# Reading the moving operand of the down products in runs from two halves

## The chip, the core and the metric

The kernel runs on one core of one Trainium2 chip. The metric is the device time of one execution in microseconds (us): lower is better. TensorE (PE in the profile) does the matrix products, with its weight loads shown apart as PEld; VectorE is DVE, ScalarE is ACT, and SyncE (SP) issues the loads from HBM.

## The reference

The reference sends 256 tokens of width 1024 through two models of two layers each. Each layer of the first has a feed-forward block, an attention mixer and a second feed-forward block; each layer of the second has a mixer (a recurrence, a retention and a spatial gate) and a feed-forward block with a causal convolution of width 3. The change touches the last product of each feed-forward block:

```python
def swiglu(x, w_gate, w_up, w_down):
    return (jax.nn.silu(x @ w_gate) * (x @ w_up)) @ w_down

def conv_ffn(h, w_up, conv_w, conv_b, w_down):
    u = h @ w_up                                   # width 2 * 2816
    c = conv_b + sum(conv_w[j] * shifted(u, j))    # three shifts along the tokens
    gate, val = jnp.split(c, 2, axis=-1)
    return (jax.nn.silu(gate) * val) @ w_down      # (256, 2816) @ (2816, 1024)
```

(The sum over the shifts is shortened here.) There are four blocks of the first kind and two of the second. All values are float32.

## The kernel before

`ffn_phase` is one feed-forward block, plain or convolutional (then `conv` is given). Both matrices are cut along the 2816 hidden units into 11 chunks of 256 units. For each chunk, `hidden` (lines 528 to 547) computes gate and up for its 2 x 128 units and all 256 tokens, with the weights stationary and the 256 tokens moving. `down` multiplies the chunk's activations by its 256 rows of the down weights: 128 tokens are stationary, 512 of the 1024 output columns move. It adds into four PSUM banks, `acc[t][half]`, for 2 blocks of 128 tokens and 2 halves of 512 output columns; they stay open over all 11 chunks. VectorE adds the finished banks to the residual `x`.

Every product is done three times, since float32 operands are split in a rounded high part and a low part of the type float32r: high x high, high x low, low x high. That is `matmul3`, lines 85 to 91, so nearly all matmuls of the profile carry the line L89, L90 or L91. Each of the three loads its stationary operand again. A chunk has 2 x 2 x 8 x 3 = 96 matmuls of 256 columns in `hidden` and 2 x 2 x 2 x 3 = 24 of 512 columns in `down`. With 6 blocks of 11 chunks there are 6336 of the first and 1584 of the second (1056 in the plain blocks, 528 in the convolutional).

The order on each engine is the order of the code. TensorE does `hidden` of chunk i + 1 and then `down` of chunk i. ScalarE makes the high parts of arrived weights (L348 gate and up, L358 down) and the activation function (L363), VectorE the low parts (L426, L443) and the product (L462 to L466). SyncE loads the next chunk as soon as the buffer that its weights first arrive in is free. TensorE waits in `down` for `down_split` and `act_ready`, which VectorE counts up.

A float32 value takes 4 bytes, so 512 moving columns are 2048 bytes in a row of one partition of SBUF, and the result is 2048 bytes in a row, a whole PSUM bank of the partition. The addresses of the operands differ between the plain blocks and the convolutional ones.

Of the kernel before, what the change touches and what calls it, by code (L numbers as in the profile page):

```python
# [84 lines left out]
def matmul3(pe, out, lhs, rhs, start, stop):  # L85

    pe.matmul(out, lhs[0], rhs[0], start=start, stop=False)  # L89
    pe.matmul(out, lhs[0], rhs[1], start=False, stop=False)  # L90
    return pe.matmul(out, lhs[1], rhs[0], start=False, stop=stop)  # L91
# [69 lines left out]
def turn_tensor(pe, c, banks, ph):  # L161

    for b in range(2 * NT):
        t, k0 = b // 2, (b % 2) * 4
        if ph.prev and t:
            keep_clock(pe, c, 2 if b % 2 else 9)
        pe.wait_ge(ph.s["h_ready"], ph.n0["h_ready"] + b + 1)
        for k in range(k0, k0 + 4):
            last = pe.transpose(c.ps[banks[b]][:, (k - k0) * P:(k - k0 + 1) * P], c.h[:, t, k * P:(k + 1) * P], c.ident)
        last.then_inc(ph.s["turned"], 1)  # L170
    if ph.prev:
        keep_clock(pe, c, 4)
# [85 lines left out]
def ffn_phase(nc, c, phase, mem, gain, weights, factor=0.5, conv=None, turn_banks=FIRST_BANKS, same_as=None):  # L258
# [9 lines left out]
    def split(tensor, part, slot):  # L268
        return tuple((tensor[slot][lo][part] if part < 2 else tensor[lo][slot]).rearrange(
            "p (k n) -> p k n", k=KT if part < 2 else 2) for lo in range(2))  # L270

    w = [[split(mem.parts if part < 2 else mem.down_parts, part, slot) for slot in range(2)] for part in range(3)]
    hT = (hT_parts[:, 0], hT_parts[:, 1])
    act_high, act_low = act_parts[:, 0], act_parts[:, 1]
# [6 lines left out]
    acc = [[c.ps[4 + 2 * t + half] for half in range(2)] for t in range(NT)]  # L281
# [242 lines left out]
    def tensor(pe):  # L524
        if ph.start:
            ph.start.shared_ready(pe)
        turn_tensor(pe, c, turn_banks, ph)

        def hidden(i, slot, first=False):
            for f in range(2):  # L530
                bank = c.ps[2 * slot + f]
                for part in range(2):
                    if first and not ph.prev and f == 0:

                        pe.wait_ge(s["gu_split" if part else "first_low"], n0["gu_split" if part else "first_low"] + 1)
                    elif first and not ph.prev:
                        pe.wait_ge(s["gu_split"], n0["gu_split"] + 2)
                    else:
                        pe.wait_ge(s["gu_split"], n0["gu_split"] + i * 2 + part + 1)
                    high, low = w[part][slot]  # L540
                    for k in range(KT):
                        if first and f == 0 and part == 0 and k in (0, KT // 2):
                            pe.wait_ge(s["hT_ready"], n0["hT_ready"] + (3 if k == 0 else 4))
                        last = matmul3(pe, bank[:, part * S:(part + 1) * S],
                                       (high[:, k, f * P:(f + 1) * P], low[:, k, f * P:(f + 1) * P]),
                                       (hT[0][:, k, :], hT[1][:, k, :]), k == 0, k == KT - 1)
                last.then_inc(s["hidden_ready"], 1)

        def down_bank(slot, f, t, half, start, stop):
            toks, cols = slice(t * P, (t + 1) * P), slice(half * 512, half * 512 + 512)  # L550
            return matmul3(pe, acc[t][half][:], (act_high[:, slot, f, toks], act_low[:, slot, f, toks]),
                           tuple(part[:, f, cols] for part in w[2][slot]), start, stop)

        def down(i, slot, first=False):
            pe.wait_ge(s["down_split"], n0["down_split"] + i + 1)
            for f in range(2):
                pe.wait_ge(s["act_ready"], n0["act_ready"] + i * 2 + f + 1)
                for t in range(NT):
                    for half in range(2):
                        last = down_bank(slot, f, t, half, first and f == 0, False)  # L560
            last.then_inc(s["down_done"], 1)

        hidden(0, 0, first=True)
        hidden(1, 1)
        down(0, 0, first=True)
        hidden(2, 0)
        down(1, 1)
        with pe.Fori(0, LOOPS - 1) as i:
            hidden(i * 2 + LOOP0, 1)
            down(i * 2 + LOOP0 - 1, 0)  # L570
            hidden(i * 2 + LOOP0 + 1, 0)
            down(i * 2 + LOOP0, 1)
        hidden(LAST - 1, 1)
        down(LAST - 2, 0)
        hidden(LAST, 0)

        pe.wait_ge(s["down_split"], n0["down_split"] + LAST)
        pe.wait_ge(s["act_ready"], n0["act_ready"] + 2 * LAST)
        for t in range(NT if conv is not None else 1):
            for half in range(2):  # L580
                for f in range(2):
                    down_bank(1, f, t, half, False, False)
        pe.wait_ge(s["down_split"], n0["down_split"] + N_CHUNK)
        pe.wait_ge(s["act_ready"], n0["act_ready"] + 2 * N_CHUNK)
        for half in range(2):
            down_bank(0, 0, 0, half, False, False)
            down_bank(0, 1, 0, half, False, True).then_inc(s["bank_done"], 1)
        for half in range(2):
            for f in range(2 if conv is None else 0):
                down_bank(1, f, 1, half, False, False)  # L590
            down_bank(0, 0, 1, half, False, False)
            down_bank(0, 1, 1, half, False, True).then_inc(s["bank_done"], 1)
# [2532 lines left out]
```

## Time and profile before

| | |
|---|---|
| median of 2 runs | 2106.91 us |
| the two runs | 2101.57 and 2112.26 us |
| span of the profiled execution | 2101.1 us |
| its own time | not listed apart; the lower of the two runs is 0.5 us above this span |
| TensorE busy | 2028.2 us, 97% of the span |
| VectorE / ScalarE busy | 1339.4 us (64%) / 998.9 us (48%) |
| mean granted TensorE clock | 0.995 of full speed (2.4 GHz) |
| moved by DMA | 348.94 MB, mean 166 GB/s |

The page counts a matmul as busy from its start to its modelled end. Matmuls overlap in TensorE: the next starts before the one before has ended. What a matmul costs in a dense stretch is thus the distance from its start to the next start, which the timeline shows, and not its duration, which the groups of lines show.

### The profile page before, as it was taken

Reading aid. Unit: us, or ns where it says so; the run is one execution under the profiler, and the core shown is the slowest. Engines: PE = TensorE matmul, PEld = TensorE weight load, DVE = VectorE, ACT = ScalarE, POOL = GpSimd, SP = SyncE. Lnnn points to the kernel's source line nnn. Section 1 sums busy time; section 2 is a strip of 40 time slices with the busy share of each in tenths; the row PEclk is TensorE's granted clock in tenths of the full one; section 3 lists DMA queues with packets and bytes.
Section 4 is the critical chain, followed back from the end, with each engine's and each line's share of the span. In section 5 each row is a group of like instructions: output and inputs, shape, how many; then the busy total and the mean of one; then the engine's idle time right before and its main releaser. Section 6 shows DMA issues by size and latency. Waiting matters only on the chain. (4 is left out here: it accounts for less than half of the span.)

```text
span 2101.1 us, 41794 instructions
## 1 busy us (share of the span) xinstructions
PE 2028.2 (97%) x17666; PEld 1877.5 (89%) x17666; DVE 1339.4 (64%) x1985; ACT 998.9 (48%) x1433; POOL 13.0 (1%) x12
## 2 busy tenths in 40 slices
PE   7999999999999999999999989999999999999997
PEld 7999987999999998799989979989998989988997
DVE  6555565754655466575547666577776856577775
ACT  5334456533543345554336544465545544456443
POOL 0000000000000000000000010000000010000000
PEclk9999999999999999999999999999999999999999
DMA  7543731554454362265344324366544333457541
GB/s 301 198 182 111 248 115 77 224 207 162 179 235 184 130 228 81 82 243 206 140 165 173 118 88 142 110 241 235 197 151 151 141 96 112 126 159 272 198 180 51
DMA packets 79878, 348.94 MB, mean 166 GB/s; under 512 B 21232, under 2 KB 30576, under 8 KB 45808
## 3 DMA queue, kind: packets, MB, share of 16 engines
q1 hardware_dynamic: 79728, 346.74, 45.1%
q8 instruction: 118, 1.93, 0.4%
q14 instruction: 32, 0.26, 0.0%
HBM read 345.67 MB, written 1.05 MB: 165 GB/s over the span
## 5 line engine op out<-in xcount | busy, mean ns | idle before, releaser
L89 PE MATMUL bank<-ffn_hT_split,n_split_gate_up 128*128 128x256 f32 x1408 | 391.3, 278 | 2.8 <-DVE ffn_hT_split L199 2.4
L90 PE MATMUL bank<-ffn_hT_split,n_split_gate_up 128*128 128x256 f32 x1408 | 390.7, 277 | 0.0
L91 PE MATMUL bank<-ffn_hT_split,n_split_gate_up 128*128 128x256 f32 x1408 | 390.6, 277 | 0.0
L89 PEld LDWEIGHTS bank<-ffn_hT_split,n_split_gate_up 128*128 128x128 f32 x1408 | 266.1, 189 | 5.2 <-issue 3.6
L90 PEld LDWEIGHTS bank<-ffn_hT_split,n_split_gate_up 128*128 128x128 f32 x1408 | 265.7, 189 | 1.5
L91 PEld LDWEIGHTS bank<-ffn_hT_split,n_split_gate_up 128*128 128x128 f32 x1408 | 265.5, 189 | 0.0
L363 ACT ACTIVATE work<-bank 128x256 f32<-128x256 f32 x88 | 33.3, 383 | 311.2 <-PE bank L91 311.2
L1814 DVE TENSOR_TENSOR mix_parts<-mix_arrived,mix_parts 128x1024 fp32r<-128x1024 f32 x88 | 107.5, 1223 | 93.4 <-ACT mix_parts L1809 93.3
L462 DVE TENSOR_TENSOR work<-bank,work 128x256 f32<-128x256 f32 x88 | 37.2, 423 | 190.2 <-ACT work L363 190.2
L443 DVE TENSOR_TENSOR ffn_split_down<-ffn_arrived_down,ffn_split_down 128x2048 fp32r<-128x2048 f32 x44 | 100.8, 2291 | 81.0 <-ACT ffn_split_down L358 81.0
L426 DVE TENSOR_TENSOR n_split_gate_up<-arrived_gate_up,n_split_gate_up 128x2048 fp32r<-128x2048 f32 x64 | 144.4, 2286 | 9.5 <-ACT n_split_gate_up L348 9.5
L1809 ACT ACTIVATE mix_parts<-mix_arrived 128x1024 fp32r<-128x1024 f32 x88 | 92.9, 1057 | 102.8 <-PE bank L91 100.5
L91 PE MATMUL bank<-ffn_split_down,ffn_act_split 128*128 128x512 f32 x352 | 138.7, 394 | 0.0
L90 PE MATMUL bank<-ffn_split_down,ffn_act_split 128*128 128x512 f32 x352 | 138.1, 392 | 0.0
L89 PE MATMUL bank<-ffn_split_down,ffn_act_split 128*128 128x512 f32 x352 | 136.8, 389 | 0.0
L358 ACT ACTIVATE ffn_split_down<-ffn_arrived_down 128x2048 fp32r<-128x2048 f32 x44 | 84.6, 1924 | 107.5 <-PE bank L91 107.0
L654 DVE TENSOR_TENSOR mixer_parts<-mixer_arrived,mixer_parts 128x512 fp32r<-128x512 f32 (+2 forms) x74 | 80.0, 1084 | 75.6 <-ACT mixer_parts L647 75.4
L348 ACT ACTIVATE n_split_gate_up<-arrived_gate_up 128x2048 fp32r<-128x2048 f32 x64 | 120.2, 1909 | 0.7 <-DMA arrived_gate_up<-in_ffn 0.6
L89 PE MATMUL bank<-normed_T_parts,mix_parts 128*128 128x256 f32 x384 | 109.8, 286 | 3.5 <-ACT inverse_T L2294 3.5
L91 PE MATMUL bank<-conv_ffn_hT_split,n_split_gate_up 128*128 128x256 f32 x384 | 106.4, 277 | 0.0
L90 PE MATMUL bank<-normed_T_parts,mix_parts 128*128 128x256 f32 x384 | 106.3, 277 | 0.0
L91 PE MATMUL bank<-normed_T_parts,mix_parts 128*128 128x256 f32 x384 | 106.3, 277 | 0.0
(393 smaller groups left out, 5711.1 us busy)
## 6 DMA issues: line engine op xcount, KB each, us to landing
arrived_gate_up<-in_ffn SPq DMA_DIRECT2D x64, 1024.0 KB, 8.5
ffn_arrived_down<-in_ffn SPq DMA_DIRECT2D x44, 1024.0 KB, 4.8
mix_arrived<-in_mix_w SPq DMA_DIRECT2D x88, 512.0 KB, 3.6
rrived_gate_up<-in_conv_ffn SPq DMA_DIRECT2D x32, 1024.0 KB, 6.8
_arrived_gate_up<-in_ffn SPq DMA_DIRECT2D x24, 1024.0 KB, 6.7
mixer_arrived<-in_w_in SPq DMA_DIRECT2D x22, 1024.0 KB, 7.2
onv_ffn_arrived_down<-in_conv_ffn SPq DMA_DIRECT2D x22, 1024.0 KB, 4.8
irst_project_arrived<-in_w_in SPq DMA_DIRECT2D x17, 1024.0 KB, 4.8
```

Source lines behind the costliest of these rows:

```text
L89: pe.matmul(out, lhs[0], rhs[0], start=start, stop=False)
L90: pe.matmul(out, lhs[0], rhs[1], start=False, stop=False)
L91: return pe.matmul(out, lhs[1], rhs[0], start=False, stop=stop)
L348: act.activation(flat(w[part][slot][0]), arrived(part, slot), ACT.Copy).then_inc(s["gu_high"], 1)
L358: act.activation(flat(w[2][slot][0]), arrived(2, slot), ACT.Copy).then_inc(s["down_high"], 1)
L363: act.activation(acts[:, slot, f], c.ps[2 * slot + f][:, 0:S], ACT.Silu).then_inc(s["silu_ready"], 1)
L426: dve.tensor_tensor(flat(low), arrived(part, slot), plain(flat(high)), ALU.subtract).then_inc(s["gu_split"], 1)
L443: dve.tensor_tensor(flat(low), arrived(2, slot), plain(flat(high)), ALU.subtract).then_inc(s["down_split"], 1)
L462: dve.tensor_tensor(value, up, value, ALU.mult).then_inc(s["product_ready"], 1)
L654: last = eng.tensor_tensor(self.parts[slot][1][:, cols], self.arrived[slot][:, cols], plain(self.parts[slot][0][:, cols]), ALU.subtract)
L1809: act.activation(self.parts[n % RING][:, 0], self.arrived[n % RING], ACT.Copy).then_inc(self.s["half_high"], 1)
L1814: dve.tensor_tensor(low, self.arrived[n % RING], plain(high), ALU.subtract).then_inc(self.s["half_split"], 1)
```

## The change

The 512 columns of the moving operand are no longer read from first to last. They are seen as two halves of 256, each half as runs of `run` columns, and are read as run 0 of the first half, run 0 of the second, run 1 of the first, run 1 of the second, and so on. The output is given the same order, so each result still lands in its own column of the bank. A run has 4 columns (16 bytes) in the plain blocks and 16 columns (64 bytes) in the convolutional ones, which makes 128 runs per matmul in the first and 32 in the second. The stationary operand, the number and order of the instructions on every engine, the waits, the loads and the arithmetic stay as they were. Only the access patterns of these 1584 matmuls differ.

```diff
+        run = 4 if conv is None else 16
+
+        def alternate(columns):
+
+            return columns.rearrange("p (a b c) -> p b a c", a=2, c=run)
+
         def down_bank(slot, f, t, half, start, stop):
             toks, cols = slice(t * P, (t + 1) * P), slice(half * 512, half * 512 + 512)
-            return matmul3(pe, acc[t][half][:], (act_high[:, slot, f, toks], act_low[:, slot, f, toks]),
-                           tuple(part[:, f, cols] for part in w[2][slot]), start, stop)
+            return matmul3(pe, alternate(acc[t][half][:]), (act_high[:, slot, f, toks], act_low[:, slot, f, toks]),
+                           tuple(alternate(part[:, f, cols]) for part in w[2][slot]), start, stop)
```

## Rows read from the trace of the kernel before

**Rows 1.** The page: span, share of each engine, granted clock.

```profile
span 2101.1 us, 41794 instructions
PE 2028.2 (97%) x17666; PEld 1877.5 (89%) x17666; DVE 1339.4 (64%) x1985; ACT 998.9 (48%) x1433; POOL 13.0 (1%) x12
PEclk9999999999999999999999999999999999999999
```

**Rows 2.** Windows: stretch, its length, busy us (instructions) of each engine, PEclk, DMA share, GB/s.

```profile
63.70:80.10 16.40, 16.40 (x121) 15.42 (x120) 9.07 (x10) 6.31 (x5) 0.00 (x0) 1.00 0.48 193
1465.80:1482.20 16.40, 16.40 (x122) 15.41 (x121) 12.11 (x18) 8.07 (x9) 0.00 (x0) 1.00 0.54 193
58.20:63.70 5.50, 5.50 (x26) 4.53 (x25) 4.20 (x5) 4.00 (x3) 0.00 (x0) 1.00 0.52 219
578.70:584.30 5.60, 5.60 (x26) 4.56 (x25) 4.31 (x5) 3.99 (x3) 0.00 (x0) 1.00 1.01 424
```

**Rows 3.** Timeline of PE, down products after hidden ones: start us, length us, instruction.

```profile
73.71 0.28 PE L90 MATMUL bank<-ffn_hT_split,n_split_gate_up 128*128 128x256 f32 x1
...
74.62 0.39 PE L89 MATMUL bank<-ffn_split_down,ffn_act_split 128*128 128x512 f32 x1
74.85 0.39 PE L90 MATMUL bank<-ffn_split_down,ffn_act_split 128*128 128x512 f32 x1
75.08 0.39 PE L91 MATMUL bank<-ffn_split_down,ffn_act_split 128*128 128x512 f32 x1
75.31 0.39 PE L89 MATMUL bank<-ffn_split_down,ffn_act_split 128*128 128x512 f32 x1
...
75.99 0.39 PE L89 MATMUL bank<-ffn_split_down,ffn_act_split 128*128 128x512 f32 x1
```

**Rows 4.** Timeline of PEld, the weight loads of two of these matmuls.

```profile
74.85 0.19 PEld L91 LDWEIGHTS bank<-ffn_split_down,ffn_act_split 128*128 128x128 f32 x1
75.08 0.19 PEld L89 LDWEIGHTS bank<-ffn_split_down,ffn_act_split 128*128 128x128 f32 x1
```

**Rows 5.** Timeline of PE, nine down products in the first chunk of another block.

```profile
580.12 0.40 PE L89 MATMUL bank<-ffn_split_down,ffn_act_split 128*128 128x512 f32 x1
...
581.99 0.40 PE L91 MATMUL bank<-ffn_split_down,ffn_act_split 128*128 128x512 f32 x1
```

**Rows 6.** Timeline of PE, seven hidden products in the same chunk.

```profile
564.82 0.28 PE L91 MATMUL bank<-ffn_hT_split,n_split_gate_up 128*128 128x256 f32 x1
...
565.52 0.28 PE L91 MATMUL bank<-ffn_hT_split,n_split_gate_up 128*128 128x256 f32 x1
```

**Rows 7.** Timeline of PE, eight products of 512 columns in the second mixer.

```profile
1389.71 0.39 PE L91 MATMUL bank<-mix_parts,merged_parts 128*128 128x512 f32 x1
...
1391.30 0.39 PE L89 MATMUL bank<-mix_parts,merged_parts 128*128 128x512 f32 x1
```

**Rows 8.** Lines of PE kept apart by shape: busy us, mean ns of one, idle before.

```profile
L91 PE MATMUL bank<-ffn_split_down,ffn_act_split 128*128 128x512 f32 x352 | 138.7, 394 | 0.0
L91 PE MATMUL bank<-conv_ffn_split_down,conv_ffn_act_split 128*128 128x512 f32 x176 | 69.4, 394 | 0.0
L97 PE MATMUL bank<-normed,w_cmp 128*64 128x30 f32 x512 | 16.5, 222 | 0.0
L97 PE MATMUL bank<-rw_v_tokens,pairs 128*64 128x64 f32 x256 | 9.9, 223 | 0.0
```

**Rows 9.** Timeline of PE, eight transposes in a row and the row after them.

```profile
200.41 1.04 PE L169 MATMUL bank<-shared_tables,normed 128*128 128x128 f32 x8
201.28 0.39 PE L155 MATMUL bank<-shared_tables 128*128 128x128 f32 x2
```

## The prediction, made before the changed kernel ran

> **What bounds the kernel now.** I read the page first. TensorE is busy 97% of the span and its clock is granted in full in every slice, so the granted level is 2.4 GHz [rows 1]. A share over the span hides stages, so I took the windows next, one whole chunk of a plain block (96 hidden and 24 down products) and one of a convolutional block. Both last 16.40 us, TensorE has no gap in either, VectorE works 9.07 and 12.11 us of them and ScalarE 6.31 and 8.07 [rows 2]. So in the stage that the change touches only TensorE decides, and there are 66 such chunks: 66 x 16.40 = 1082 us, half of the span. The last view is the timeline, for the pace inside it.
>
> The pace has to be read from start to start. Six down products start in 75.99 - 74.62 = 1.37 us, and the window of the 24 has 5.50 us: 229 ns each, though each shows 0.39 us of its own [rows 2, 3]. Eight hidden products of 256 columns take 74.62 - 73.71 = 0.91 us, 114 ns each [rows 3]. At 2.4 GHz and one column per cycle 512 columns are 213.3 ns and 256 are 106.7. A down product thus pays 229 - 213 = 15.7 ns that its columns do not explain, a hidden one about 7. The weight load of the next product starts with each matmul and has 0.19 us to show, less than the 0.23 us between starts [rows 3, 4], so the loads do not set the pace of the down products. No VectorE or ScalarE work does either: the pace of a chunk's 24 products is one number while those engines start and stop.
>
> **The extra time is not a constant.** This is what I rest the forecast on. In the first chunk of another block nine down products stand 1.87 us apart over eight steps, 234 ns each [rows 5]; that whole window has 5.60 us instead of 5.50 [rows 2]. The hidden products before it stand 0.70 / 6 = 117 ns apart instead of 114 [rows 6]. The mixer's products of the same 512 columns take 1.59 / 7 = 227 ns [rows 7]. One shape, one clock, no idle time, and 227, 229 or 234 ns: so something in how the two operand streams fall together adds 14 to 20 ns. A change of the order of addresses acts on just that, in one direction or the other.
>
> **The change, part by part.** No instruction is added, removed or moved, no wait and no load changes. 1584 matmuls get another order of reading and writing, and nothing covers them: TensorE is the bound, so each ns saved or lost per matmul is 1.58 us of the kernel. If TensorE gets faster, VectorE is the next bound at 9.07 or 12.11 of 16.40 us, and it would take a gain of 4 us per chunk to meet it, more than the whole gain possible; the loads run at 193 GB/s in these chunks against 424 in the busiest window here [rows 2], so they follow too. If TensorE gets slower, everything else waits.
>
> *Columns.* The clock still passes one column per cycle: the lower end is 213.3 ns. The whole gain possible is 1584 x 15.7 ns = 24.8 us, 1.2%.
>
> *Reading and writing in runs.* No dense stretch before has it. The nearest rows are two. The compressing products have 30 moving columns, read and written as two runs of 15, and last 222 ns, where the contiguous 64 columns last 223 [rows 8]. By columns they should be 34 / 2.4 = 14 ns shorter and are 1 ns shorter, so a jump may hide up to 13 ns there, or the duration has a floor; one jump in a sparse stretch can't tell. The other row is the slowest pace at which TensorE takes columns at full clock here: eight float32 transposes of 128 columns in 0.87 us, 109 ns each, 0.85 ns per column [rows 9], which is 435 ns for 512. So a down product lies between 213 and 435 ns, a change of between -25 and 1584 x 206 ns = +326 us.
>
> Between these I take the value by the nearest rows, the products of the same shape. They move by 2 ns down and 5 ns up when the operands' places alone change [rows 5, 7]. Alternating two places is a larger change of the same kind. A run of 4 float32 is read from one place before the other is touched, so successive groups never lie next to each other; if the extra comes from successive reads meeting, about half of it should go. I take 8 of the 15.7 ns: 221 ns. That gives 1584 x 8 = -12.7 us, 8.4 in the plain and 4.2 in the convolutional blocks. That it is half is a choice, with 0 and 15.7 as its ends.
>
> *Sum.* The profiled span of 2101.1 us stands 0.5 us under the lower run shown, 2101.6, and the median of the two is 5.3 us above that. 2101.6 - 12.7 = 2088.9 for a run like the profiled one; I add half of the 5.3 us for the run's own spread: **2091.5 us**.
>
> *A rule that speaks against the change.* The rows show contiguous output only in the products of 512 columns, at 227 to 234 ns [rows 5, 7]. The Trainium skill, "PSUM — Partial Sum Buffer", section "Specifications (TRN2)", says that PSUM has lines of 8 bytes and that any non-contiguous pattern slows matmuls significantly. It gives no price, and the sum above goes without it. Read by its lines alone the rule would be silent here, since runs of 4 and of 16 float32 fill whole lines; read by its words it is the second or third rival below. No run so far shows which.
>
> **The rivals.**
>
> 1. *Nothing to gain (28%).* The extra 15.7 ns comes from the pairing of weight load and matmul and not from the order of the columns, and a jump is free. For it: the extra per matmul stays the same within a chunk in spite of all other work. Against it: a hidden product has the same weight load and half the extra, as if it went with the columns. The time is that of before, 2100 to 2112 us.
>
> 2. *A jump costs a cycle (9%, slower).* Each change of half holds the stream by one column, 0.42 ns. There are 1056 x 128 + 528 x 32 = 152,064 runs, so +63 us: about 2165 us. The price per run decides: 42 us are 2% of the time, so from 0.28 ns per run the kernel is slower by over 2%. A plain down product would stand at 229 + 53 = 282 ns and a convolutional one at 242. For it: the two-run product that is no shorter than one of twice its columns [rows 8]. Against it: in contiguous reading, too, the address moves on all the time, at 0.45 ns per column.
>
> 3. *Writing or reading in pieces halves the pace (6%, slower).* Down products at the transposes' pace, 435 ns [rows 9], in both kinds of block: 2101.6 + 326 = 2428 us. This is what the PSUM page's sentence taken by its words would most look like. Against it in the rows there is only that the two-run product shows no such price [rows 8].
>
> 4. *The slower footing spreads (5%).* The 234 and 117 ns of one chunk [rows 5, 6] are a way in which the pair of streams can run, entered there and left at the next chunk. If the new pattern leads into it everywhere, the down products cost 1584 x 4.5 = 7 us and the 6336 hidden ones at 3.5 ns 22 us: 2101.6 + 29 = 2131 us.
>
> **How the numbers follow.** The forecast, some part of the extra gone, has 52%; it covers 2076.8 (all 24.8 us gone) to about 2100. With rival 1 it makes 80%, so the range reaches from 2076 to 2118: the upper end holds the upper run of before, 2112, and a small price of the jumps, up to 0.1 ns each. The rest, 20%, is beyond it. About 2%, or 42 us, is what a measurement of this kernel tells from no change. No case gives a gain of 2%; I keep 2% for an error in the reading of the pace. Rivals 2 and 3 are slower by more, 15%. Within 2% is all else, 83%.
>
> **What would show it.** Right: the down products stand about 221 ns apart in the timeline, the windows of 24 have 5.3 us and not 5.5, a chunk 16.2 and not 16.4, and the hidden products stay at 114. Rival 1: 229 again. Rival 2: 282 in the plain and 242 in the convolutional blocks. Rival 3: over 400 in both. Rival 4: 117 between hidden products of all chunks. The prediction is wrong in its main step if the pace of the down products rises or does not move, and in its size if it falls to 214 or only to 227.

## The result: slower by 1.8%, and the profile after

The changed kernel takes 2142.34 us, in both of its runs. Against the kernel before that is a ratio of 1.0182, with a 95% interval of 1.0162 to 1.0202 (the quotient of the two medians shown is 1.0168, inside it). The forecast was 2091.5 us, in a range up to 2118. The page of the profile, the answer to [rows 1]:

```profile
span 2140.6 us, 41794 instructions
PE 2068.3 (97%) x17666; PEld 1892.8 (88%) x17666; DVE 1339.7 (63%) x1985; ACT 1003.4 (47%) x1433; POOL 13.0 (1%) x12
PEclk9999999999999999999999999999999999999999
```

The span is 39.5 us longer and TensorE is busy 40.1 us longer, with the same instructions, the clock still granted in full, and VectorE's work unchanged. So the time went into TensorE's own pace. The windows of three whole chunks and of three stretches in them stand against [rows 2]: two chunks of a plain block that follow each other, a convolutional one, then 24 down products, and the hidden products of the two plain chunks.

```profile
64.10:81.00 16.90, 16.90 (x122) 15.45 (x121) 8.99 (x10) 6.44 (x5) 0.00 (x0) 1.00 0.47 187
81.00:98.30 17.30, 17.30 (x121) 15.86 (x120) 9.06 (x10) 6.42 (x5) 0.00 (x0) 1.00 0.46 182
1477.00:1494.10 17.10, 17.10 (x123) 15.92 (x122) 12.14 (x18) 8.06 (x9) 0.00 (x0) 1.00 0.50 186
75.00:81.00 6.00, 6.00 (x27) 4.55 (x26) 4.66 (x5) 4.12 (x3) 0.00 (x0) 1.00 0.49 205
64.10:75.00 10.90, 10.90 (x98) 10.90 (x96) 4.33 (x5) 2.31 (x2) 0.00 (x0) 1.00 0.46 177
81.00:92.30 11.30, 11.30 (x98) 11.30 (x97) 4.42 (x5) 2.31 (x2) 0.00 (x0) 1.00 0.48 185
```

A chunk of 16.40 us became 16.9, 17.3 or 17.1 us, and TensorE has no gap in any. Two things are to be seen. The down products of a plain chunk take 6.00 us instead of 5.50. And the hidden products, which the change does not touch, take 10.90 us in one chunk and 11.30 in the next.

The timeline of PE gives the paces. First plain down products, eight steps in 1.99 us, 249 ns each, where [rows 3] had 229:

```profile
75.00 0.41 PE L89 MATMUL bank<-ffn_split_down,ffn_act_split 128*128 128x512 f32 x1
...
76.99 0.42 PE L91 MATMUL bank<-ffn_split_down,ffn_act_split 128*128 128x512 f32 x1
```

Then convolutional ones, eight steps in 1.92 us, 240 ns each:

```profile
1477.73 0.40 PE L89 MATMUL bank<-conv_ffn_split_down,conv_ffn_act_split 128*128 128x512 f32 x1
...
1479.65 0.40 PE L91 MATMUL bank<-conv_ffn_split_down,conv_ffn_act_split 128*128 128x512 f32 x1
```

And hidden products of the second plain chunk above, nine steps in 1.06 us, 118 ns each. Before, this pace stood only in a few chunks, as in [rows 6]:

```profile
84.75 0.28 PE L91 MATMUL bank<-ffn_hT_split,n_split_gate_up 128*128 128x256 f32 x1
...
85.81 0.28 PE L91 MATMUL bank<-ffn_hT_split,n_split_gate_up 128*128 128x256 f32 x1
```

Summed over all starts of the two traces, start to next start:

| matmuls | before, us | after, us | difference |
|---|---|---|---|
| 1056 down, plain | 242.6 | 264.7 | +22.1 |
| 528 down, convolutional | 121.3 | 126.8 | +5.5 |
| 4224 hidden, plain | 484.2 | 489.7 | +5.6 |
| 2112 hidden, convolutional | 241.7 | 249.0 | +7.3 |

That is 40.5 us, the span's 39.5 within 1 us. Two thirds are the products that were changed; a third are their untouched neighbours.

### The profile page after: what moved, and what is told of

Read it like the earlier page. It is cut to its first block and busy times, and to the rows that moved or that the text cites. A ratio compares the mean times of both kernels' runs of the same rounds, so it can differ in the third digit from the quotient of the medians.

```text
span 2140.6 us, 41794 instructions
## 1 busy us (share of the span) xinstructions
PE 2068.3 (97%) x17666; PEld 1892.8 (88%) x17666; DVE 1339.7 (63%) x1985; ACT 1003.4 (47%) x1433; POOL 13.0 (1%) x12
## 5 line engine op out<-in xcount | busy, mean ns | idle before, releaser
L90 PE MATMUL bank<-ffn_split_down,ffn_act_split 128*128 128x512 f32 x352 | 146.8, 417 | 0.0
L91 PE MATMUL bank<-ffn_split_down,ffn_act_split 128*128 128x512 f32 x352 | 146.8, 417 | 0.0
L89 PE MATMUL bank<-ffn_split_down,ffn_act_split 128*128 128x512 f32 x352 | 144.8, 411 | 0.0
L358 ACT ACTIVATE ffn_split_down<-ffn_arrived_down 128x2048 fp32r<-128x2048 f32 x44 | 84.7, 1925 | 122.1 <-PE bank L91 121.3
```

The source lines that it names most:

```text
L358: act.activation(flat(w[2][slot][0]), arrived(2, slot), ACT.Copy).then_inc(s["down_high"], 1)
```

## The experiments

The two theories to tell apart were: the stream read out of SBUF is held, or the results written to PSUM are. Mean paces below are over 24 down products or 96 hidden ones, taken from the starts. "Loop chunks" are the 9 of each block's 11 chunks whose hidden products follow down products: 36 in the plain blocks and 18 in the convolutional ones. All experiments change the kernel with the change in it. Each ratio is the recorded one to the kernel before, run beside it, whose median was 2105.7 us for the first four experiments on record (e1 to e4), 2104.13 us for e5 to e8 and 2105.82 us for e9 to e12; it can differ in the third decimal from the quotient of the medians.

**Reading in runs, writing in one piece (e1).**

```diff
-            return matmul3(pe, alternate(acc[t][half][:]), (...
+            return matmul3(pe, acc[t][half][:], (...
```

> Only the moving operand is read in runs from two halves; the results are written in one piece, so the columns of each bank come out permuted and the output is not the reference's. Reading theory (the stream out of SBUF is held at jumps): the pace of the changed kernel stays, 251 ns plain and 240 ns convolutional between down products, about 2142 us. Writing theory (PSUM is held at jumps): back to 229 ns in both, about 2104 us. If both sides share the price, something between, near 2120 us.

Measured: 2145.93 us, ratio 1.0184 (1.0152 to 1.0217). Eight steps of the timeline take 2.00 us, 250 ns, and the convolutional products stand at 240.

```profile
75.94 0.41 PE L89 MATMUL bank<-ffn_split_down,ffn_act_split 128*128 128x512 f32 x1
...
77.94 0.42 PE L91 MATMUL bank<-ffn_split_down,ffn_act_split 128*128 128x512 f32 x1
```

**Writing in runs, reading in one piece (e2).**

```diff
-                           tuple(alternate(part[:, f, cols]) for part in w[2][slot]), start, stop)
+                           tuple(part[:, f, cols] for part in w[2][slot]), start, stop)
```

> Only the results are written in runs to two halves; the moving operand is read in one piece, so columns come out permuted and the output is not the reference's. Writing theory: 251 and 240 ns, about 2142 us. Reading theory: 229 ns in both, about 2104 us. In either case the hidden products, whose patterns are untouched, show whether their pace (113.6 or 117.9 ns) hangs on the side that is changed.

Measured: 2108.6 us, ratio 0.9999 (0.997 to 1.0028). Eight steps take 1.83 us, 229 ns:

```profile
74.69 0.39 PE L89 MATMUL bank<-ffn_split_down,ffn_act_split 128*128 128x512 f32 x1
...
76.52 0.39 PE L91 MATMUL bank<-ffn_split_down,ffn_act_split 128*128 128x512 f32 x1
```

The price in the down products' own pace is on the reading side: writing in runs of 4 or 16 columns leaves it at 228.9 ns, but for one of the two convolutional blocks, where it is 229.7 to 229.8. In that block the hidden products of all nine loop chunks stand at 117.8 ns; in the other, with the same order, they stand at 113.6. The window of 96 hidden products in the slow block:

```profile
1440.10:1451.40 11.30, 11.30 (x97) 11.30 (x96) 9.21 (x11) 7.04 (x7) 0.00 (x0) 1.00 0.60 228
```

In all, the hidden products of the convolutional blocks take 3.6 us more than in the kernel before, too little to show in the ratio. The Trainium skill, "PSUM — Partial Sum Buffer", section "Specifications (TRN2)", says that any non-contiguous pattern slows matmuls significantly. For these runs, which fill its 8-byte lines, the measurement decides against it as far as the pace of the written products goes.

**Longer runs: 64 in both kinds of block (e3)** (`run = 64`).

> Runs of 64 columns in both kinds of block: 8 runs per product instead of 128 and 32. If each jump has its price (0.17 ns in the plain, 0.35 ns in the convolutional blocks by the changed kernel), at most 3 ns over 229: 232 ns, about 2109 us. If a product that jumps at all loses a fixed amount, 240 ns stay, about 2125 us or more. If the reading of two places is what costs and the length of a run is not, 240 to 251 ns.

Measured: 2103.04 us, ratio 1.0003 (0.998 to 1.0025); 228.9 ns in both kinds, here in a plain block, eight steps in 1.83 us:

```profile
74.28 0.39 PE L89 MATMUL bank<-ffn_split_down,ffn_act_split 128*128 128x512 f32 x1
...
76.11 0.39 PE L91 MATMUL bank<-ffn_split_down,ffn_act_split 128*128 128x512 f32 x1
```

Reading from two places is free when each run is 256 bytes.

**The run lengths swapped (e4)** (`run = 16 if conv is None else 4`).

> Run lengths swapped: 16 in the plain blocks, 4 in the convolutional ones. If the length of the run sets the pace: 240 ns plain and 251 ns convolutional, about 11 us x 1 less in the plain and 6 us more in the convolutional blocks, near 2137 us. If the operands' addresses in the two kinds of block set it: plain stays near 251 and convolutional near 240.

Measured: 2142.85 us, ratio 1.0169 (1.0138 to 1.0201). Plain 240.0 ns, convolutional 249.0 and 252.0 ns in turn, mean 250.5. Between the two kinds of block the length of the run sets the pace and their addresses don't. Here all 36 plain loop chunks have hidden products at 118 ns, so the total missed the expected 2137 us: the hidden products of both kinds together took 2.9 us more than in the changed kernel.

**Runs of 8 and 32 (e8)** (`run = 8 if conv is None else 32`) **and of 2 and 128 (e11)** (`run = 2 if conv is None else 128`).

> Runs of 8 columns in the plain blocks and of 32 in the convolutional ones, to complete the curve of 4, 16 and 64 columns (251, 240, 229 ns). If the price is one of each jump with some of it hidden, between the neighbours: about 245 ns for 8 and 234 ns for 32. If a run of 16 or less loses a fixed 11 ns and the run of 4 another effect on top: 240 for 8 and 229 for 32.

> Ends of the curve: runs of 2 columns (8 bytes) in the plain blocks and of 128 in the convolutional ones. By the curve so far (251, 243, 240, 237, 229 ns for 4, 8, 16, 32, 64 columns) 128 gives 229 ns. For 2 columns: if each 16 bytes are now fetched twice and fetching has little slack, well over 300 ns and above 2200 us; if only the number of jumps counts at the price between 8 and 4 columns (about 0.11 ns each), 265 ns and about 2160 us.

Measured: 2126.44 us (ratio 1.011, 1.0054 to 1.0166) and, in a single run, 2220.07 us against 2103.46 to 2108.19 of the kernel before beside it. With runs of 2 the plain products stand 340 ns apart; eight steps of the timeline take 2.72 us:

```profile
78.57 0.51 PE L90 MATMUL bank<-ffn_split_down,ffn_act_split 128*128 128x512 f32 x1
...
81.29 0.51 PE L89 MATMUL bank<-ffn_split_down,ffn_act_split 128*128 128x512 f32 x1
```

| run, columns | 2 | 4 | 8 | 16 | 32 | 64 | 128 | in one piece |
|---|---|---|---|---|---|---|---|---|
| runs per product | 256 | 128 | 64 | 32 | 16 | 8 | 4 | 1 |
| ns per product | 340 | 250.5 | 243.4 | 240.0 | 236.7 | 228.9 | 229 | 228.9 |
| over one piece, per run | 0.43 | 0.17 | 0.23 | 0.35 | 0.49 | 0 | 0 | |

There is no price per jump: halving the run from 64 to 32 adds 8 ns for 8 more runs, from 32 to 4 only 14 ns for 112 more. A step stands between 64 and 32 columns and a much larger one between 4 and 2, where a run gets shorter than 16 bytes. These are runs from two halves; from four places, below, 16 columns cost less.

**What the 16 bytes do (e9).** Plain blocks read the same 16 bytes 128 times, convolutional ones go forward as before but take the four columns of each 16 bytes in the order 0, 2, 1, 3.

```diff
+            def moving(part, f, half):
+                if conv is None:
+                    return part[:, f, half * 512:half * 512 + 4].unsqueeze(1).to_broadcast([P, 128, 4])
+                return part[:, f, cols].rearrange("p (b a c) -> p b c a", a=2, c=2)
```

> Results are written in one piece, only the reading differs, and the output is not the reference's. Plain blocks: the same 4 columns (16 bytes) are read 128 times over, so the moving operand never moves on. Convolutional blocks: the reading stays in order from one 16 bytes to the next, but within them the columns are taken as 0, 2, 1, 3. If the extra 15.7 ns of the kernel before come from fetching ever new 16-byte pieces: plain falls to 214 to 217 ns. If they belong to the matmul or to its weight load: plain stays at 229 ns. If a jump costs wherever it goes: convolutional above 251 ns (256 jumps or more). If only leaving a 16-byte piece out of order costs: convolutional stays at 229 ns.

Measured in one run: 216 ns plain, 229 ns convolutional, each as expected if fetching ever new pieces is what costs. First the timeline of plain products, nine steps in 1.95 us, then of convolutional ones, eight in 1.83:

```profile
72.16 0.38 PE L89 MATMUL bank<-ffn_split_down,ffn_act_split 128*128 128x512 f32 x1
...
74.11 0.38 PE L89 MATMUL bank<-ffn_split_down,ffn_act_split 128*128 128x512 f32 x1
```

```profile
1486.34 0.39 PE L89 MATMUL bank<-conv_ffn_split_down,conv_ffn_act_split 128*128 128x512 f32 x1
...
1488.17 0.39 PE L91 MATMUL bank<-conv_ffn_split_down,conv_ffn_act_split 128*128 128x512 f32 x1
```

13 of the 15.7 ns that a down product pays over its columns are the price of moving on through SBUF, even in order; 2.7 ns remain when it does not move on. Order within 16 bytes is free. This price alone isn't what the runs of 4 to 32 pay: they visit as many 16-byte pieces per product as reading in order, 128, and cost 8 to 22 ns more. Why leaving the order costs stays open. The Trainium skill, "SBUF — State Buffer", section "Door 1: The DMA port swizzle", names lines of 16 bytes and a penalty for crossing to a new one; these two paces and the step below 4 columns agree. It also has full bandwidth from two accesses per line on, and there the measurement differs: runs of 2 columns have two and stand at 340 ns.

The total did not move: 2106.21 us beside 2103.46 to 2108.19. The windows of this kernel, first 96 hidden products and then the 24 down products before them, show where 13.6 us went:

```profile
77.34:88.65 11.31, 11.31 (x97) 11.30 (x96) 5.16 (x5) 2.31 (x2) 0.00 (x0) 1.00 0.51 188
72.16:77.34 5.18, 5.18 (x26) 4.54 (x25) 3.91 (x5) 3.98 (x3) 0.00 (x0) 1.00 0.47 196
```

The down products gain 0.32 us per chunk. The hidden ones, now at 117.8 ns in all 36 loop chunks of the plain blocks, give 0.4 us back.

**Less weight to load beside the stream (e7).** 64 stationary columns in place of 128 in nearly all down products, plain blocks reading in one piece, convolutional in runs of 16.

```diff
+            rows = P if start or stop else DH
+            toks = slice(t * P, t * P + rows)
+            order = (lambda columns: columns) if conv is None else alternate
```

> The stationary operand of the down products has 64 columns instead of 128 (but for the first f of the first chunk and the last product), so only 64 of 128 tokens of each block are computed and the output is not the reference's. The moving operand is read in one piece in the plain blocks and in runs of 16 in the convolutional ones. If the 15.7 ns over the columns, and the 11 ns more in runs, come from the weight load that runs beside the reading: with half of the load about half of both goes, 221 ns plain and 227 convolutional, down products 1056 x 8 + 528 x 13 = 15 us less than in the changed kernel's convolutional and the kernel before's plain blocks. If they belong to the reading of the moving operand alone: 229 and 240 ns stay, about 2113 us.

Measured: 2124.88 us (ratio 1.0103, 1.0042 to 1.0164) where 2113 were expected; 228.9 ns plain and 239.8 to 240.1 convolutional, so the pace is the same with half of the stationary columns. The load's own rows fell from 188 to 134 ns (in the page's shape 128x64):

```profile
L90 PEld LDWEIGHTS bank<-ffn_split_down,ffn_act_split 128*64 128x64 f32 x320 | 43.0, 134 | 26.9
```

Neither the extra of the contiguous products nor that of the runs shrinks with the weight load; and on the same 16 bytes 216 ns were reached beside full loads, whose rows show 189 ns. But the hidden products went to 117.8 ns in 34 of 36 plain loop chunks, though the down products before them read in one piece. In all the hidden products take 16.4 us more than in the kernel before, which is what the expectation left out.

**Other distances and numbers of places (e5 and e10).** Two experiments. First runs of 16 from 4 places 512 bytes apart (plain) and 16 places 128 bytes apart (convolutional): `places = 4 if conv is None else 16`, with `a=places`. Then two places 1088 and 1040 bytes apart, read only:

```diff
+            def moving(part, f, half):
+                first, apart = f * 1024 + half * 448, 272 if conv is None else 260
+                flat_part = part.rearrange("p k n -> p (k n)")[:, first:first + 2 * apart]
+                places = flat_part.rearrange("p (a x) -> p a x", a=2)[:, :, 0:256]
+                return places.rearrange("p a (b c) -> p b a c", c=16)
```

> Runs of 16 columns as in the slow form, read and written in turn from 4 places 512 bytes apart in the plain blocks and from 16 places 128 bytes apart in the convolutional ones (instead of 2 places 1024 bytes apart). If only the length of the run counts, every jump having its price whatever its width: 240 ns in both, about 2143 us. If the distance of 1024 bytes is what makes two successive reads meet: near 229 ns in both, about 2105 us. If jumps to a near address are free and far ones not: 240 plain, 229 convolutional.

> Reading in runs of 16 in turn from two places, written in one piece, output not the reference's. The places are 1088 bytes apart in the plain blocks and 1040 in the convolutional ones, instead of 1024. If two places a multiple of 1024 bytes apart meet in the memory: 229 ns plain (shifted by 64 bytes) and, if the grain is 16 bytes, 229 ns convolutional too. If the price is that of a jump out of order: 240 ns in both.

Measured: 2118.95 us (ratio 1.0075, 1.0037 to 1.0113) with 233.3 and 235.2 ns in turn plain and 240.2 convolutional; then 240.0 and 240.1 ns, 2115.25 us in one run. So 1024 bytes are nothing special: 128, 1040 and 1088 give the same 240. Four places 512 bytes apart give 5 to 7 ns less, which none of the theories explains; no run tells the number of places from their distance.

**The neighbours' pace (e6).** The last 3 of the 24 products of a chunk read and write in one piece again:

```diff
+            order = (lambda columns: columns) if f and t and half else alternate
```

> The changed kernel, but the last three of the 24 down products of a chunk (second f, second token block, second half; three of each slot's last bank) read and write in one piece. The slow pace of the hidden products after them (117.9 ns in all chunks of the convolutional blocks, in every second of the plain ones) is tested. If the last products before the hidden ones set their footing: hidden products back to 113.6 ns in all loop chunks, 13 us less by them, and 1584/8 = 198 products at 229 instead of 251 or 240, 3.6 us less: about 2126 us. If the footing is set by the group as a whole or by the length of the chunk: only the 3.6 us, about 2139 us.

Measured: 2132.38 us, ratio 1.0138 (1.0089 to 1.0188). The expectation held for one kind of block only. Windows of 96 hidden products, plain and then convolutional:

```profile
80.00:90.88 10.88, 10.88 (x97) 10.88 (x96) 4.49 (x5) 2.32 (x2) 0.00 (x0) 1.00 0.49 178
1473.15:1484.45 11.30, 11.30 (x97) 11.30 (x96) 8.96 (x10) 7.04 (x7) 0.00 (x0) 1.00 0.34 128
```

All 36 plain loop chunks are at 113.4 ns. All 18 convolutional ones stay at 117.8.

The traces show a little more of this. With runs of 4, a group of 24 down products behind hidden ones at 113.6 ns takes 249.0 ns each and the hidden ones behind it go to 117.9; a group behind 117.9 takes 252.0, and the next hidden ones are back at 113.6. This holds for every such group of the changed kernel (36), of the read-only one (36), of the one changed in the plain blocks alone (36) and of the swapped one (18), also where a block starts on the other pace. So these groups swap the two paces, which is why every second plain chunk is slow. In the kernel before, the down products always end at the fast pace: behind first chunks at 118 ns they take 233.3 ns once, and in all loop chunks after that the paces are 113.6 and 228.9.

**The change in the plain blocks alone (e12)** (`run = 4 if conv is None else 256`).

> The change in the plain blocks alone; in the convolutional ones the run is 256, which is the old order. If the loss is the sum of what the two kinds of block show in the trace (plain 22.1 us of down and 5.6 us of hidden products, convolutional 5.5 and 7.3 us), about 28 of the 39.5 us stay: a ratio near 1.013 to the kernel before. If the footing of one block is handed on to the next, more than that is left.

Measured: 2134.06 us, ratio 1.0134 (1.0068 to 1.02), as the sum of the parts has it, in a wide interval. The convolutional down products are back at 229 ns, their hidden ones at 113.6.

## Why the prediction was wrong

**What bounds the kernel** held. TensorE is the bound in these stages, its start-to-start pace is the measure, nothing covers it, and the clock is full: each added ns came out as time (40.5 us of starts, 39.5 us of span).

**The step that failed** is the one that took about half of the extra 15.7 ns off, "if the extra comes from successive reads meeting". I had seen that the extra varies with the operands' places and took that for a sign that another order could lower it. Nothing showed that successive reads meet. 13 ns of the extra vanish when the stream stays on the same 16 bytes, so they are the price of moving on through SBUF, and every order that covers the 512 columns has to move on. None tried is cheaper than in order; runs of 64 and more and a shuffle within 16 bytes are level with it, and all others add. In place of 8 ns less the plain products pay 22 ns more and the convolutional ones 11. The forecast for them was -12.7 us, and they made +27.6.

**Rival 2**, a price per jump, had the side and the place right and the size wrong. A cycle per run would have been 282 and 242 ns and +63 us. The convolutional value nearly fits, which is chance: the table of runs shows that the price does not count jumps. I gave it 9%. Its evidence, the two-run product that is no shorter than one of twice its columns [rows 8], was not tested; the up to 13 ns per jump that it allowed are far from the 0.17 to 0.49 measured.

**Rival 3**, half the pace from writing or reading in pieces, did not occur: no pace came near 435 ns, and reading alone carries the price of the down products.

**Rival 4**, the slower footing, came in part and on top of the rest. 38 of the 54 loop chunks (20 plain, 18 convolutional) went to it: 38 x 96 x 4.25 ns = 15.5 us, against 12.9 us net in the hidden rows of the table, since some first chunks got faster. I had priced it as an alternative to the others, at 3.5 ns per hidden product instead of 4.25; it was a second term of the same outcome.

**Rival 1** is refuted by both parts: a jump is not free, and the extra neither shrinks with the weight load nor stays when the stream stands on 16 bytes.

**The range** reached up to a price of 0.1 ns per run. The two paces amount to 0.17 and 0.35 ns, and the neighbours' 13 us were not in the sum that gave the forecast and its range.

**What stays open.** Why the hidden products take one of two paces, 113.6 or 117.8 ns, is not settled. It is not set by the pace of the down products before them: 240 ns go with 117.8 in one kernel and with 113.5 in another, 229 ns with both. The order of the down products before them and the pace before those decide together in runs of 4, but the same order left one convolutional block slow and the other fast in the write-only kernel. Three last products in one piece brought the fast pace back in the plain blocks and not in the convolutional. Nor is it known why leaving the order costs at all, why the step lies between runs of 32 and 64, or why four places are cheaper than two. No kernel tried beats the one before: runs of 64 columns are level with it.

## What to carry to other kernels

When float32r matmuls run back to back, read the moving operand in order, or in runs of at least 64 columns, which cost nothing here; writing the results to PSUM in runs of 4 or 16 changed the pace of the products that write by 1 ns at most. An unexplained rest above the column count is a limit to be tested by removing its supposed cause (one experiment on the same 16 bytes) before an order is built on it. And sum the neighbours too: a change of one group's pace can move a group it never touches, and give a gain back.

## What the runs showed of the hardware that was not expected

- A moving stream that never leaves 16 bytes takes 216 ns for 512 columns at the full clock, in order 229, in runs of 16 columns 240, in runs of 2 columns 340.
- Untouched matmuls of 256 columns have two steady paces, 113.6 and 117.8 ns, each held for a whole chunk of 96. A gain of 13.6 us in the products before them was fully given back through it, in one run.
- Down products in runs of 4 turn one of these two paces into the other, group by group, which makes every second chunk slow.
- Half of the stationary columns shorten a weight load from 188 to 134 ns and leave the matmul's pace at 229 ns.
